# Constants multiplied during TensorE's waits, weight staging moved into the heads' norm, and an output projection in three float32r products

## The chip, the cores and the metric

One core of one Trainium2 chip runs the whole program. The metric is the device time of one execution in microseconds (us). TensorE (PE) multiplies, VectorE (DVE), ScalarE (ACT) and GpSimd (POOL) compute elementwise, SyncE (SP) and also ACT and POOL issue transfers (DMA). TensorE's clock has two levels, 2.4 GHz and 1.2 GHz; the profile's PEclk is the granted share, 1.00 for the first and 0.50 for the second.

## What is computed

Two blocks, one after the other, in float32, on one sequence of 512 tokens of width 1024.

```python
# first block
proj = rmsnorm(x, attn_norm_g) @ w_in
sb_out = stick_breaking_attention(q, k, v)           # 8 heads of 64
d_out = differential_attention(rope(norm(dq)), rope(norm(dk)), dv, lam)   # 4 heads of 2 x 64
d_out = rmsnorm(d_out, diff_subln_g, 1e-5) * 0.8     # norm of each head: lambda_init is 0.2
x = x + concatenate([sb_out, d_out]) @ w_o
h2 = rmsnorm(x, ffn_norm_g)
x = x + (silu(h2 @ w_gate) * (h2 @ w_up)) @ w_down   # hidden width 2816
# second block, on 16 meta tokens and the 512 of x
proj = rms_norm(h) @ w_in_2                          # 72 tiles of 1024 x 128, and dt
branch_conf = silu(layer_norm(conv31(a * sigmoid(g)))) @ w_conf_out
branch_ssm = rms_norm(bidir_ssd(silu(conv7(xbc)), dt) * silu(z)) @ w_ssm_out
h = h + (gate1 * branch_conf + gate2 * branch_ssm) @ w_out
h = h + expert_choice_ffn(rms_norm(h))               # 16 experts, 66 tokens each
out = rms_norm(h[16:])
```

## The kernel before

The order on every engine is written out by hand: a block of Python for each engine issues its instructions one after the other, and semaphores tie them together. An engine works strictly in its written order, so whatever stands behind a waiting instruction waits too.

**A product in float32r.** Most dense products split both operands into a high part (rounded to float32r by an ACT copy) and a low part (raw minus high, by DVE), and TensorE multiplies high by high, high by low and low by high: three passes of one matmul each. `ffn_high` and `ffn_low` do this for the pieces of `w_gate`, `w_up` and `w_down`; `split_piece` (L783, L784, L787) multiplies them. The output projection `wo` (L758) still multiplies plain float32: 8 output tiles m by 8 tiles k, 64 matmuls of 512 columns, from the ring slots 2 and 3 that hold `w_o`, and `MIX`, the heads' outputs.

**Attention.** The stick-breaking heads run as a pipeline over i: scores (L598) of head i, the sums over later keys `("c", i-1)` (L687), the rotation of a rope tile (L699), the output `("o", i-2)` (L714). Between them ACT takes logarithms, DVE subtracts (L1895), POOL masks (L2443) and makes the cosine part (L2456). Then 4 differential heads of 4 query blocks run through scores (L672), softmax on DVE and ACT, transposes (L727) and outputs (L737). Then comes the norm of each head: ACT squares (L1387), PE sums with ones (L748, `subln_sum`), ACT takes the root (L1379, L1381, `subln_root`), DVE scales `MIX` (L1947). In this part PE multiplies the four stick-breaking tiles k = 0 to 3 of output tiles m = 0 to 3 between the sums, and waits for the semaphore `mix_ready` before k = 4 to 7.

**Staging of the second block's weights.** 72 tiles of `w_proj` (512 KB each) are read by POOL's queue (`pre_load`, L2477) into one of 3 buffers, split by ACT (`pre_high`, L1413) and DVE (`pre_low`, L1962), and the low part is written to DRAM by POOL's queue (L2484) for later. This is spread over the first block by tables: `PRE_WO` says how many tiles follow each output tile m of the output projection (6 in all), `PRE_GATE` 2 for each of 22 hidden tiles, `PRE_DOWN` after which pieces of `w_down` (22 of the pieces 3 to 31). POOL issues the first three loads once all heads are normed; afterwards it stores tile q and then loads tile q+2 into the buffer of tile q-1, once that one's store has landed. Before the first FFN weight is split, ACT waits for all tiles of `PRE_WO`, since both use the buffers `WF`. SP's queue loads the big weight blocks (2 MB each) into the ring: the first block of `w_gate`/`w_up` once output tile 3 is done, the second once tile 7 is.

**Second block.** `norm_total("n3")` (L583) sums squares, the dt product follows (L828), then the 72 projection tiles (`split_proj`, L841) among the conformer's taps (DVE L2133, L2082, kept in order with ACT's `conf_gate` L1502, L1506), and for each of 4 groups g the scan over 5 chunks c: `ob` (L978), `of` (L983), `yd` (L988), `sf` (L994), `turn_y` (L925). After the last chunk the dense tail begins: `so` (L1023, L1028), `co`, `out`. The expert part (L1155) ends the program.

```python
            for m in range(DT):
                if m < 4:
                    subln_sum(m)
                wo(m, range(0, 4 if m < 4 else DT))
                if m == 3:
                    pe.wait_ge(S("mix_ready"), DIFF_HEADS)
                    for j in range(4):
                        wo(j, range(4, DT))
```

## Time and profile before

| | |
|---|---|
| median of 3 runs | 2572.95 us (2569.82 to 2579.66) |
| the profiled execution's own time | 2572.31 us |
| its span | 2570.3 us |
| mean granted clock of TensorE | 0.978 |
| busy: PE, DVE, ACT, POOL | 2439.2 us (95%), 1607.2 us (63%), 821.3 us (32%), 406.6 us (16%) |

The span runs from the first to the last instruction of the profiled execution. Times in the rows are microseconds from its start. A float32 matmul shows as two records, a float32r one as one, and matmuls overlap in their records, so the rate of a row of matmuls is read from starts or from the chain of work, not from their mean duration. "Idle before" names what ended the wait of an engine.

### The profile page before, as it was taken

Reading aid. Unit: us, or ns where it says so; the run is one execution under the profiler, and the core shown is the slowest. Engines: PE = TensorE matmul, PEld = TensorE weight load, DVE = VectorE, ACT = ScalarE, POOL = GpSimd, SP = SyncE. Lnnn points to the kernel's source line nnn. Section 1 sums busy time; section 2 is a strip of 40 time slices with the busy share of each in tenths; the row PEclk is TensorE's granted clock in tenths of the full one; section 3 lists DMA queues with packets and bytes.
Section 4 is the critical chain, followed back from the end, with each engine's and each line's share of the span. In section 5 each row is a group of like instructions: output and inputs, shape, how many; then the busy total and the mean of one; then the engine's idle time right before and its main releaser. Section 6 shows DMA issues by size and latency. Waiting matters only on the chain.

```text
span 2570.3 us, 41027 instructions
## 1 busy us (share of the span) xinstructions
PE 2439.2 (95%) x17615; PEld 1541.8 (60%) x17615; DVE 1607.2 (63%) x1749; ACT 821.3 (32%) x1361; POOL 406.6 (16%) x423
## 2 busy tenths in 40 slices
PE   8998899999989999999989989999999999999996
PEld 6764468887879898989879973333322333232322
DVE  4346456664538898988484641766666666666664
ACT  3256544443444646464454421000100000000001
POOL 0033012111202212123330400100000000111110
PEclk9999999999989999999989999999999999999998
DMA  5200168878846454546523468999999999999996
GB/s 201 83 33 1 53 233 296 293 280 283 283 168 201 140 199 148 191 154 210 168 94 116 172 254 308 368 410 414 412 412 412 412 412 415 414 413 411 411 412 233
DMA packets 129717, 676.31 MB, mean 263 GB/s; under 512 B 19300, under 2 KB 52068, under 8 KB 100228
## 3 DMA queue, kind: packets, MB, share of 16 engines
q1 hardware_dynamic: 56624, 554.81, 54.3%
q0 software_dynamic: 25632, 88.49, 10.2%
q10 hardware_dynamic: 47284, 30.42, 4.4%
q8 instruction: 140, 2.29, 0.4%
q14 instruction: 37, 0.30, 0.0%
HBM read 618.55 MB, written 55.12 MB: 262 GB/s over the span
## 4 chain that ended last, share of the span: by engine, by line
PE 66%; DMA 19%; DVE 7%; ACT 4%; issue 2%; POOL 1%; ACTq 0%; SPq 0%; POOLq 0%; DVEq 0%
PE PS L1155 24%; DMA expert_ring_high<-w_experts 12%; PE PS L841 11%; PE PS L1023 5%; DMA arena<-w_proj 3%; PE PS L787 3%; PE PS L783 3%; PE PS L784 3%; PE PS L1028 2%; PE PS L758 2%; DMA ring<-ssd_sums 2%; ACT ring L1562 2%; PE PS L687 1%; PE PS L634 1%; PE PS L635 1%
## 5 line engine op out<-in xcount | busy, mean ns | idle before, releaser
L1155 PE MATMUL PS<-expert_ring_high,U 128*32 128x512 f32 x4240 | 472.2, 596 | 17.5 <-DMA expert_ring_high<-w_experts 16.8
L1155 PE MATMUL PS<-expert_ring_low,U 128*32 128x512 f32 x4016 | 447.1, 593 | 10.7 <-DMA expert_ring_low<-w_experts 8.9
L841 PE MATMUL PS<-XH,RINGF 128*128 128x264 f32 x2304 | 392.4, 289 | 1.2 <-ACT arena L1506 1.2
L1155 PEld LDWEIGHTS PS<-expert_ring_high,U 128*32 128x32 f32 x4240 | 136.2, 110 | 328.4 <-issue 302.6
L841 PEld LDWEIGHTS PS<-XH,RINGF 128*128 128x128 f32 x2304 | 324.3, 189 | 9.2 <-issue 6.8
L1155 PEld LDWEIGHTS PS<-expert_ring_low,U 128*32 128x32 f32 x4016 | 128.7, 110 | 309.4 <-issue 289.7
L2349 DVE SCALAR_TENSOR_TENSOR arena<-expert_ring_low,U,arena 128x2048 f32<-128x2048 f32 x134 | 305.7, 2345 | 0.0
L841 PE MATMUL PS<-UH,RINGF 128*128 128x264 f32 x1152 | 233.7, 285 | 0.0
L2082 DVE SCALAR_TENSOR_TENSOR H<-arena,par,H 128x528 f32<-128x528 f32 x240 | 186.7, 821 | 1.3
L841 PEld LDWEIGHTS PS<-UH,RINGF 128*128 128x128 f32 x1152 | 179.4, 189 | 0.0
L2349 DVE SCALAR_TENSOR_TENSOR arena<-expert_ring_high,U,arena 128x2048 f32<-128x2048 f32 x76 | 174.0, 2347 | 0.5
L2588 POOL DMA_INDIRECT residual_rows<-H,scatter_rows x16 | 29.6, 1851 | 849.2 <-DVE H L2380 849.2
L1772 ACT ACTIVATE H<-PS 128x512 f32<-128x512 f32 x32 | 19.1, 597 | 407.0 <-PE PS L1155 407.0
L1962 DVE TENSOR_TENSOR PREL<-arena,PS 128x1024 fp32r<-128x1024 f32 x66 | 80.4, 1219 | 98.8 <-ACT PS L1413 98.6
L783 PE MATMUL PS<-UX,WF 128*128 128x512 f32 x352 | 138.5, 393 | 0.8 <-DVE UX L1818 0.8
L784 PE MATMUL PS<-UX,WF 128*128 128x512 f32 x352 | 137.1, 389 | 0.0
L2133 DVE SCALAR_TENSOR_TENSOR SQ<-arena,par,SQ 128x528 f32<-128x528 f32 x144 | 109.6, 766 | 6.3 <-ACT SQ L1494 3.7
L2496 POOL TENSOR_TENSOR arena<-arena,ring 128x512 f32<-128x512 f32 (+1 forms) x32 | 60.6, 1898 | 317.5 <-ACT arena L1587 257.7
L1782 ACT ACTIVATE SQ<-PS 2x512 f32<-2x512 f32 x32 | 18.9, 591 | 271.6 <-PE PS L1155 271.2
L1413 ACT ACTIVATE PS<-arena 128x1024 fp32r<-128x1024 f32 x66 | 67.7, 1025 | 116.7 <-DMA arena<-w_proj 114.8
L2358 DVE TENSOR_TENSOR H<-H,PS 128x512 f32<-128x512 f32 x32 | 22.0, 688 | 125.4 <-ACT H L1772 87.2
L1397 ACT ACTIVATE WF<-ring 128x1024 fp32r<-128x1024 f32 (+1 forms) x76 | 71.4, 942 | 80.8 <-PE PS L787 80.1
(358 smaller groups left out, 3898.1 us busy)
## 6 DMA issues: line engine op xcount, KB each, us to landing
expert_ring_low<-w_experts SPq DMA_DIRECT2D x96, 2048.0 KB
expert_ring_high<-w_experts SPq DMA_DIRECT2D x96, 2048.0 KB, 30.0
arena<-w_proj POOLq DMA_DIRECT2D x72, 512.0 KB, 5.6
projection_low_parts<-PREL POOLq DMA_DIRECT2D x72, 512.0 KB, 4.2
ring<-w_proj SPq DMA_DIRECT2D x72, 512.0 KB, 3.7
RINGF<-projection_low_parts SPq DMA_DIRECT2D x72, 512.0 KB, 4.6
ring<-w_gu SPq DMA_DIRECT2D x11, 2048.0 KB, 10.2
ring<-ssd_sums ACTq DMA_DIRECT2D x32, 512.0 KB, 8.5
```

Of the source, the lines that this page charges most:

```text
L783: nc.tensor.matmul(PS[:, bank, :], hi[:, k, :], src[:, 0, k0 + k, :], start=(start and k == 0), stop=False)
L784: nc.tensor.matmul(PS[:, bank, :], hi[:, k, :], src[:, 1, k0 + k, :], start=False, stop=False)
L787: last = nc.tensor.matmul(PS[:, bank, :], lo[:, k, :], src[:, 0, k0 + k, :], start=False, stop=(stop and k == n - 1))
L841: last = nc.tensor.matmul(PS[:, banks[i], 0:HT], w[:, k, :], x[:, k, lo:hi], start=start, stop=stop)
L1023: nc.tensor.matmul(PS[:, banks[i], 0:HT], wh[:, k, :], x(k)[:, lo:hi], start=(first and k == 0 and x is high), stop=False)
L1155: mm = nc.tensor.matmul(PS[QUAD * t:QUAD * t + QUAD, bank, :], stat(t), move(t), start=start, stop=stop)
L1397: A(split_high(p), raw(p), ACT.Copy).then_inc(S("weights_high"), 1)
L1413: A(pre_high_place(q), pre_raw(q), ACT.Copy).then_inc(S("pre_high"), 1)
L1962: V_.tensor_tensor(PREL[:, q % STAGE, :], pre_raw(q), pre_high_place(q).bitcast(F32), SUB).then_inc(S("pre_low"), 1)
L2082: ins = V_.scalar_tensor_tensor(acc, CP[:, u % 3, j:j + T2], par[:, w0 + j:w0 + j + 1], acc, MUL, ADD)
L2133: V_.scalar_tensor_tensor(co, xp[:, k:k + T2], par[:, w0 + k:w0 + k + 1], co, MUL, ADD)\
L2349: ins = V_.scalar_tensor_tensor(LACC[:, a, :], w, XG[:, k, a:a + 1], LACC[:, a, :], MUL, ADD)
```

## The change

1. `fill_wait(bank, n, width)` multiplies `ones` by the constants, n times, in plain float32, into a bank that the next real product overwrites. It stands ahead of a wait at: the sums `("c", 0)` and `("c", 7)` (2 of 512 columns each), `("o", 7)`, the first transposes of the differential heads, every one of their 16 outputs (4, 1, 1, 2 of 128 columns by query block), the first norm of a head, `n3` (5 of 512), dt (2 of 512), `sf` of chunk 0 of groups 1 and 2 (4 and 1 of 256), in group 3 `ob` of chunk 0 (3 of 256) and `yd` (3, 0, 0, 4, 8 of 256 by chunk), ahead of the last `turn_y`, the first `so` (4 of 512) and the first `out`. To allow this `open_` (the wait for the bank) moves ahead of the wait for the operand.
2. The output projection becomes three float32r products. ACT and DVE split the 8 tiles of `w_o` in the stick-breaking loop, one for each head, and `MIX` in 8 tiles: k = 0 to 3 in the last differential head, k = 4 to 7 in the heads' norm. Roots of the heads' norm get other rows, since the split tiles lie where they were.
3. Four staged tiles are split in the heads' norm, and `PRE_WO` keeps 6, so 10 tiles come before the FFN; `PRE_DOWN` has 18 instead of 22, and none after pieces 30 and 31. POOL issues the first three loads after the last stick-breaking scores, and for the first 10 tiles it loads tile q+3 right after the store of tile q, once that store has landed.
4. `conf(1, 0)` (one projection tile) moves from behind the dt sums F, TOT and FR to ahead of them.

```diff
+PRE_HEADS = 4
+PRE_WO = [1, 1, 2, 2, 0, 0, 0, 0]
 PRE_GATE = [2] * FFT
+PRE_DOWN = [n for n in range(3, 31) if n % 3 != 0]
+N_PRE_WO = PRE_HEADS + sum(PRE_WO)
...
+            def fill_wait(bank, n, at=0, width=512):
+                for _ in range(n):
+                    nc.tensor.matmul(PS[:, bank, at:at + width], ones, consts[:, 0:width], start=True, stop=True)
...
                 if 1 <= i <= SB_HEADS:
                     h = i - 1
+                    open_(("c", h), 3, 4, 5)
+                    if h in (0, SB_HEADS - 1):
+                        fill_wait(3, 2)
                     pe.wait_ge(S("sp_masked"), 4 * h + 1)
-                    open_(("c", h), 3, 4, 5)
...
             def wo(m, ks):
+                hi, lo = wo_high(m), wo_low(m)
                 if ks.start == 0:
+                    pe.wait_ge(S("weights_low"), WO_W + m + 1)
                     open_(("wo", m), m % 4)
                 for k in ks:
-                    last = nc.tensor.matmul(PS[:, m % 4, :], w[:, k, (m % 4) * P:(m % 4) * P + P], MIX[:, k, :],
-                                            start=(k == 0), stop=(k == DT - 1))
+                    if m == 0:
+                        pe.wait_ge(S("x_low"), MIX_X + k + 1)
+                    nc.tensor.matmul(PS[:, m % 4, :], hi[:, k, :], mix_high(k), start=(k == 0), stop=False)
+                    nc.tensor.matmul(PS[:, m % 4, :], hi[:, k, :], mix_low(k), start=False, stop=False)
+                    last = nc.tensor.matmul(PS[:, m % 4, :], lo[:, k, :], mix_high(k), start=False, stop=(k == DT - 1))
...
# ACT, stick-breaking loop and heads' norm
+                    act.wait_ge(*in_used[23])
+                    A(wo_high(i), wo_raw(i), ACT.Copy).then_inc(S("weights_high"), 1)
...
                 if h >= 1:
                     subln_root(h - 1)
+                    pre_high(1)
             subln_root(DIFF_HEADS - 1)
+            pre_high(PRE_HEADS - DIFF_HEADS + 1)
...
+            for h in range(DIFF_HEADS):
+                act.wait_ge(S("mix_ready"), h + 1)
+                A(mix_high(4 + h), MIX[:, 4 + h, :], ACT.Copy).then_inc(S("x_high"), 1)
...
# DVE, stick-breaking loop and heads' norm
+                    dve.wait_ge(S("weights_high"), WO_W + i + 1)
+                    if i < SB_HEADS - 1:
+                        dve.wait_ge(S("cos_part"), i + 2)
+                    V_.tensor_tensor(wo_low(i), wo_raw(i), wo_high(i).bitcast(F32), SUB).then_inc(S("weights_low"), 1)
...
             for h in range(DIFF_HEADS):
                 dve.wait_ge(S("head_rooted"), 8 + h + 1)
+                R = HEAD_ROOT[h]
                 V_.scalar_tensor_tensor(MIX[:, 4 + h, :], MIX[:, 4 + h, :], small[:, 5:6], R, MUL, MUL).then_inc(S("mix_ready"), 1)
+                if h >= 1:
+                    mix_rest(4 + h - 1)
+                if h < DIFF_HEADS - 1:
+                    pre_low(1)
+            mix_rest(4 + DIFF_HEADS - 1)
+            pre_low(1)
...
# POOL
-            pool.wait_ge(S("mix_ready"), DIFF_HEADS)
+            got(pool, ("z", SB_HEADS - 1))
...
-                if 1 <= q <= N_PROJ - STAGE:
+                if q < N_PRE_WO:
+                    pre_load(q + STAGE)
+                elif N_PRE_WO < q <= N_PROJ - STAGE:
                     pre_load(q + STAGE - 1)
```

`mix_rest(k)` waits for ACT's high part of tile k and subtracts it from `MIX` on DVE.

**DVE in the heads' norm.** Of the kernel before, from the last differential map on (L1947 scales a head, L1962 makes the low part of a staged tile, L1968 adds an output tile to H):

```order
L1931 SCALAR_TENSOR_TENSOR arena<-arena,small 128x512
L1947 SCALAR_TENSOR_TENSOR arena<-arena,small 128x512 x4
L1968 TENSOR_TENSOR H<-H,PS 128x512 x2
L1818 SCALAR_TENSOR_TENSOR UX<-H,par,UX 128x512
L1962 TENSOR_TENSOR PREL<-arena,WF 128x1024
```

Of the change, the same place (L2033 scales a head, L1985 is `mix_rest`, L2027 the low part of a staged tile, L2051 adds to H):

```order
L2006 SCALAR_TENSOR_TENSOR arena<-arena,small 128x512
L2033 SCALAR_TENSOR_TENSOR arena<-arena,small 128x512
L2027 TENSOR_TENSOR PREL<-arena,WF 128x1024
L2033 SCALAR_TENSOR_TENSOR arena<-arena,small 128x512
L1985 TENSOR_TENSOR GX<-arena,GX 128x512
L2027 TENSOR_TENSOR PREL<-arena,WF 128x1024
L2033 SCALAR_TENSOR_TENSOR arena<-arena,small 128x512
L1985 TENSOR_TENSOR GX<-arena,GX 128x512
L2027 TENSOR_TENSOR PREL<-arena,WF 128x1024
L2033 SCALAR_TENSOR_TENSOR arena<-arena,small 128x512
L1985 TENSOR_TENSOR GX<-arena,GX 128x512 x2
L2027 TENSOR_TENSOR PREL<-arena,WF 128x1024
```

The first `mix_rest` stands ahead of the scaling of heads 2 and 3. Its high part comes from ACT, whose order there is:

```order
L1460 ACTIVATE SQ<-arena 128x512
L1439 ACTIVATE arena<-PS,par 128x512
L1441 ACTIVATE arena<-arena 128x512
L1453 ACTIVATE WF<-arena 128x1024
L1439 ACTIVATE arena<-PS,par 128x512
L1441 ACTIVATE arena<-arena 128x512
L1453 ACTIVATE WF<-arena 128x1024
L1481 ACTIVATE GX<-arena 128x512 x4
```

These are the last square, the root of head 2 (L1439, L1441), a staged tile (L1453), the root of head 3, the fourth staged tile, and then the four high parts of `MIX` (L1481).

**DVE at the end of `w_down`.** Of the kernel before, from piece 28 to the norm n3 (L1950 low part of a piece, L2003 and L2005 an output tile into H, L1826 adds a square):

```order
L1950 TENSOR_TENSOR RINGF<-ring,WF 128x6x128
L1950 TENSOR_TENSOR RINGF<-ring,WF 128x5x128
L1962 TENSOR_TENSOR PREL<-arena,PS 128x1024
L2003 TENSOR_TENSOR U<-PS,RS 128x512
L2005 TENSOR_TENSOR H<-H,U 128x512
L1826 TENSOR_TENSOR U<-U,SQ 128x528
```

Of the change, the same place (L2042 the pieces, L2087 and L2089 into H, L1891 the square):

```order
L2027 TENSOR_TENSOR PREL<-arena,PS 128x1024
L2042 TENSOR_TENSOR RINGF<-ring,WF 128x5x128
L2027 TENSOR_TENSOR PREL<-arena,PS 128x1024
L2042 TENSOR_TENSOR RINGF<-ring,WF 128x6x128
L2042 TENSOR_TENSOR RINGF<-ring,WF 128x5x128
L2087 TENSOR_TENSOR U<-PS,RS 128x512
L2089 TENSOR_TENSOR H<-H,U 128x512
```

No staged tile stands any more between the last two pieces and the last three output tiles.

## Rows read from the trace of the kernel before

**Rows 1.** The chain of waits that ended last, on the page: shares of the span.
```profile
PE 66%; DMA 19%; DVE 7%; ACT 4%; issue 2%; POOL 1%; ACTq 0%; SPq 0%; POOLq 0%; DVEq 0%
```

**Rows 2.** Stretches: length, busy PE, weights, DVE, ACT, POOL, PEclk, DMA share, GB/s.
```profile
156.00:180.00 24.00, 21.72 (x72) 12.71 (x72) 15.13 (x16) 12.30 (x10) 14.85 (x23) 0.86 0.00 0
240.00:286.00 46.00, 33.93 (x170) 22.22 (x171) 30.12 (x72) 31.69 (x93) 0.00 (x0) 0.85 0.00 1
299.00:344.00 45.00, 45.00 (x107) 19.96 (x106) 22.12 (x28) 18.64 (x25) 7.69 (x14) 1.00 0.58 210
380.00:400.00 20.00, 20.00 (x89) 16.48 (x88) 13.11 (x14) 10.32 (x12) 3.92 (x8) 1.00 0.85 299
640.00:660.00 20.00, 17.90 (x71) 14.58 (x72) 10.99 (x12) 8.96 (x11) 4.22 (x8) 0.91 0.82 278
700.00:740.00 40.00, 30.91 (x149) 23.02 (x148) 22.73 (x37) 19.27 (x29) 2.51 (x5) 0.87 0.62 226
980.00:1000.00 20.00, 18.03 (x117) 15.70 (x117) 14.17 (x18) 9.30 (x21) 7.26 (x7) 0.91 0.68 204
1240.00:1260.00 20.00, 17.10 (x99) 14.41 (x98) 10.98 (x13) 6.88 (x11) 5.92 (x5) 0.83 0.67 157
1290.00:1312.00 22.00, 14.12 (x71) 9.85 (x69) 11.61 (x17) 20.85 (x53) 9.09 (x8) 0.75 0.03 13
1312.00:1340.00 28.00, 23.73 (x153) 23.47 (x154) 27.75 (x29) 7.76 (x12) 11.82 (x7) 0.77 0.38 150
```

**Rows 3.** Timeline of PE and POOL, stick-breaking loop: start, duration, what, idle before.
```profile
168.60 5.92 PE L687 MATMUL PS<-arena,consts_sb 128*128 128x512 f32 x14 [2.28 <-POOL arena L2443]
...
226.81 3.09 PE L687 MATMUL PS<-arena,consts_sb 128*128 128x512 f32 x14 [2.33 <-POOL arena L2443]
...
160.12 1.76 POOL L2456 TENSOR_TENSOR U<-arena 128x512 f32<-128x512 f32 x1
...
191.23 1.28 POOL L2456 TENSOR_TENSOR U<-arena 128x512 f32<-128x512 f32 x1
```

**Rows 4.** The chain in order of time, output projection: start, duration, records.
```profile
299.29 44.65 PE PS L758 x104
```

**Rows 5.** Timeline of ACT and DVE in the output projection.
```profile
308.12 1.04 ACT L1413 ACTIVATE WF<-arena 128x1024 fp32r<-128x1024 f32 x1
...
326.97 1.06 ACT L1413 ACTIVATE WF<-arena 128x1024 fp32r<-128x1024 f32 x1 [11.95 <-DMA arena<-w_proj]
...
311.09 1.22 DVE L1962 TENSOR_TENSOR PREL<-arena,WF 128x1024 fp32r<-128x1024 f32 x1
...
343.96 0.69 DVE L1968 TENSOR_TENSOR H<-H,PS 128x512 f32<-128x512 f32 x1 [0.42 <-PE PS L758]
...
347.09 0.74 DVE L1818 SCALAR_TENSOR_TENSOR UX<-H,par,UX 128x512 fp32r<-128x512 f32 x1
```

**Rows 6.** Landing times from 300 to 420 us of L2484 (stores), then L2477 (loads).
```profile
DMA to landing us min/median/max: 2.9/4.9/10.7
...
DMA to landing us min/median/max: 3.7/4.9/11.4
```

**Rows 7.** Timeline of PE and DVE, `w_down` to the dt product.
```profile
642.10 0.67 PE L783 MATMUL PS<-GX,WF 128*128 128x512 f32 x1 [2.42 <-ACT WF L1397]
...
718.70 2.10 PE L583 MATMUL PS<-U,consts_sb 128*128 128x264 f32 x4 [6.14 <-DVE U L1826]
723.17 9.50 PE L828 MATMUL PS<-U,arena 128*64 128x264 f32 x32 [2.36 <-DVE U L2012]
...
710.69 1.22 DVE L1962 TENSOR_TENSOR PREL<-arena,PS 128x1024 fp32r<-128x1024 f32 x1 [3.88 <-ACT PS L1413]
```

**Rows 8.** Timeline of ACT, the second conformer gate.
```profile
776.22 0.61 ACT L1502 ACTIVATE RS<-PS 128x528 f32<-128x528 f32 x1 [3.49 <-PE PS L841]
```

**Rows 9.** Timeline of PE, last chunk of the scan and first dense tile.
```profile
1309.71 1.86 PE L988 MATMUL PS<-arena 16*16 16x64 f32 x16 [3.56 <-DVE arena L2064]
...
1332.90 0.81 PE L1023 MATMUL PS<-XH,WH 128*128 128x264 f32 x2 [3.66 <-DVE YTL L2105]
```

More of the change, by code:

```diff
@@ L99 @@
 PAIRS = 4
-PRE_WO = [1, 2, 1, 2, 0, 0, 0, 0]
+PRE_HEADS = 4
+PRE_WO = [1, 1, 2, 2, 0, 0, 0, 0]
 PRE_GATE = [2] * FFT
-PRE_DOWN = [n for n in range(3, 32) if n % 4 != 2]
-N_PRE_WO = sum(PRE_WO)
+PRE_DOWN = [n for n in range(3, 31) if n % 3 != 0]
+N_PRE_WO = PRE_HEADS + sum(PRE_WO)
 assert N_PRE_WO + sum(PRE_GATE) + len(PRE_DOWN) == N_PROJ
-FFN_W = 24
+WO_W = 24
+FFN_W = WO_W + DT
 PROJ_W = FFN_W + 2 * FFT + 32
@@ L281, in program, with mix_high, mix_low, wo_raw @@
         SUMMED = U[:, 4, 0:3 * P]
+        HEAD_ROOT = [QK[:, row, :] for row in (8, 11, 14, 15)]
+        rows = GX[:, :, :, :].rearrange("p a f n -> p (a f) n")
+        MIX_ROW, V_ROW, QK_ROW = 17, 9, 1
+        assert 2 * DT * SEQ + (FBUF + STAGE) * PIECE - DT * T2 == P + 5 * 1280 + (16 - V_ROW) * SEQ
+        def mix_high(k):
+            return rows[:, (2, 3, 5, 6)[k] if k < 4 else V_ROW + k - 4, :]
+        def mix_low(k):
+            return rows[:, MIX_ROW + k, :]
+        def wo_raw(m):
+            return slot(("wo", m // 4))[:, :, (m % 4) * P:(m % 4) * P + P]
+        def wo_high(m):
+            return WI[:, m // 4, m % 4, :].rearrange("p (k n) -> p k n", k=DT)
+        def wo_low(m):
+            return RINGF[:, slot_of[where["wo", m // 4]] - 2, :].rearrange("p (k n) -> p k n", k=DT)[:, :, (m % 4) * P:(m % 4) * P + P]
         def Z(h):
@@ L887, in _ @@
                 fill(last, ("dtT", part))
+            conf(1, 0)
             pe.wait_ge(*freed(("dtT", 0)))
@@ L905, in _ @@
             fill(last, "FR")
-            conf(1, 0)
             conf(1, 1)
@@ L1333, in _ @@
                     log_terms(i)
+                if i < SB_HEADS:
+                    name = ("wo", i // 4)
+                    act.wait_ge(S(f"ring{slot_of[where[name]]}"), landed[name])
+                    act.wait_ge(*in_used[23])
+                    A(wo_high(i), wo_raw(i), ACT.Copy).then_inc(S("weights_high"), 1)
                 if i >= 1:
@@ L1375, in _ @@
                     diff_out((n - 4) // QB - 1)
+                if 12 <= n < 16:
+                    got(act, ("s", 11))
+                    act.wait_ge(*freed(("o", 2 * (n - 12) + 1)))
+                    A(mix_high(n - 12), MIX[:, n - 12, :], ACT.Copy).then_inc(S("x_high"), 1)
             diff_out(DIFF_HEADS - 1)
@@ L1414, in pre_high, with ffn_high, hidden_high @@
                 pre_turn[0] += n
-            act.wait_ge(S("mix_ready"), DIFF_HEADS)
+            for h in range(DIFF_HEADS):
+                act.wait_ge(*freed(("do", h)))
+                if h >= 2:
+                    got(act, ("sl", h - 2))
+                A(SQ[:, h % 2, 0:SEQ], MIX[:, 4 + h, :], ACT.Square).then_inc(S("subln_sq"), 1)
+                if h >= 1:
+                    subln_root(h - 1)
+                    pre_high(1)
+            subln_root(DIFF_HEADS - 1)
+            pre_high(PRE_HEADS - DIFF_HEADS + 1)
+            def ffn_high(p):
+                name = pieces[p][0]
+                act.wait_ge(S(f"ring{slot_of[where[name]]}"), landed[name])
+                if p >= FBUF:
+                    act.wait_ge(*piece_used[p - FBUF])
+                A(split_high(p), raw(p), ACT.Copy).then_inc(S("weights_high"), 1)
+            def hidden_high(m):
+                act.wait_ge(*freed(("up", m)))
+                A(GX[:, 0, m, :], GXL[:, m, :], ACT.Copy).then_inc(S("x_high"), 1)
+            got(act, ("do", DIFF_HEADS - 1))
+            for h in range(DIFF_HEADS):
+                act.wait_ge(S("mix_ready"), h + 1)
+                A(mix_high(4 + h), MIX[:, 4 + h, :], ACT.Copy).then_inc(S("x_high"), 1)
             for m in range(DT):
```

92 lines of the change are left out of this document (50 added, 42 removed).

## The prediction

> **What bounds the kernel now.** The chain of waits comes first [rows 1]: PE holds 66% of it, then DMA 19% and DVE 7%. So one microsecond taken from PE's own work counts where PE has no wait, and nothing where it waits for another engine. Next come stretches of the span with PE's busy time and granted clock [rows 2]. What a low clock can cost is the length times (1 - PEclk): 24 x 0.14 = 3.4 us in the stick-breaking loop, 46 x 0.15 = 6.9 in the differential heads, 1.8 at 640, 5.2 at 700 to 740, 1.8 at 980, 3.4 at 1240, then 5.5 and 6.4 at the end of the scan. That ceiling is 34 us; it includes time in which PE waits anyhow. The output projection (299 to 344) is the opposite: PE is busy without a gap at full clock [rows 2], and the chain runs through it alone [rows 4]. A wait of 2.28 us at 168.6 left PE slow (14 sums in 5.92 us), a wait of 2.33 at 226.8 did not (3.09 us) [rows 3]. [...]
>
> **Prices.** The chain shows 104 records, 52 float32 matmuls of 512 columns, in 44.65 us [rows 4]: 0.859 us each at full clock, so a fill costs 0.86, 0.43 or 0.215 us for 512, 256 or 128 columns. The first FFN stretch has 89 float32r matmuls in 20.00 us without a gap [rows 2]: 0.2247 each. The sum is made against the profiled execution, 2572.31 us, which is 0.6 below the median.
>
> **1. Stick-breaking loop: +0.2.** Ahead of `("c", 0)` 1.7 us of fill stand where PE had little or no wait, and the loop runs in a circle DVE, POOL's mask, PE, so nothing behind absorbs them: +1.7. The slow sums at 168.6 cost 5.92 - 3.09 = 2.8 us [rows 3]; a fill or a shift ahead of them may save them, I take half, -1.5. The splits of `w_o` are 1.04 us of ACT and 1.22 of DVE for each head [rows 5]; ACT and DVE are busy 12.30 and 15.13 of 24 us [rows 2], so idle time covers them; without that cover each costs its whole length. Bounds: -3 (clock kept, fill hidden) and +5 (fill and half the splits on the circle).
>
> **2. Differential heads: -1.7.** PE is busy 33.93 of 46 us, so the clock cost at most 33.93 x 0.15 = 5.0 [rows 2]; DVE (30.12) and ACT (31.69) also bound the stretch. I take -3.0 for the clock, +0.3 for fills that overrun their wait, +1.0 for the splits of `MIX` tiles 0 to 3 on ACT and DVE. Bounds: -5 and 0.
>
> **3. Output projection: -0.5.** 64 x 0.859 = 55.0 us become 192 x 0.2247 = 43.1, a gain of 11.8. It is mostly given back.
> - Of it, 4 x (3.44 - 2.70) = 2.9 lies in the half products between the heads' sums, where PE waits for the norm in any case.
> - The operands of k = 4 to 7 come late. After ACT's fourth staged tile DVE must do 0.7 + 1.2 + 0.75 + 0.7 + 1.2 + 0.75 + 0.7 + 0.7 = 6.7 us (scalings, low parts, staged tiles; durations of 0.69, 1.22 and 0.74 in [rows 5]), in the order that the change's rows show, with the first low part ahead of the scalings of heads 2 and 3. PE could begin k = 4 at about 300.5 and has 2.7 us of work for the four: output tile 0 is full near 307.4, tile 3 near 315.6, tile 7 near 337.1.
> - The FFN then waits for ten staged tiles. POOL issues store q, waits until it has landed, then issues load q + 3. With the least landing of 2.9 us [rows 6] and two issues I estimate 4.3 us a tile. Store 0 goes out near 298, seven stores (0 to 6) take it to 328, load 9 lands 4.9 us later (median [rows 6]): near 333, split by 334.7. Behind that split DVE has, for the FFN's first operands, some 10.7 us (three rounds of H, operand, square and low part, and the last one). So the last operand is ready at 345.4; before it was 347.09 + 0.74 = 347.8 [rows 5]: -2.4. Before, ACT waited 11.95 us for its last staged tile and still had it by 328, and DVE waited for PE by 0.42 only [rows 5], so there the product was the bound; now the staging is.
> - PE stands idle from 337.1 to 345.4, the longest wait of the program's first part, and starts again at the lower clock: about +1.9.
>
> Bounds: -10.5 (all but the restart's part kept) and +17 (rival B).
>
> **4. `w_down`: -2.5.** Behind a staged tile PE waits 2.42 us at 642.1 and the clock falls [rows 7]; 1.8 us is the loss after it [rows 2]. Staged tiles follow 2 of 3 pieces instead of 3 of 4, so ACT gets 1 us in 12 pieces back. Bounds 0 and -4.7 (stall, clock and a little of each piece).
>
> **5. n3 and dt: -5.0.** DVE's staged tile at 710.69 (1.22 us) is gone from between the last piece and the three adds of H. PE has `w_down` finished at 718.70 - 6.14 = 712.56 and starts n3 at 718.70 [rows 7]. The squares could be added by 715.4, but the five fills take 5 x 0.859 = 4.3 and hold PE to 716.8: -1.9. At full clock n3 itself takes 1.0 less. The dt product takes 9.50 for 16 matmuls [rows 7]; at full clock one of 264 columns takes 0.859 x 264/512 = 0.44, and 16 x 0.44 = 7.0: up to -2.4, of which I take 2.1. Bounds -1.9 and -5.5.
>
> **6. `conf(1, 0)` ahead of F, TOT and FR: +0.7.** One tile is 8 tiles k, three passes and two halves of 264 columns, 48 matmuls, 48 x 0.2247 x 264/512 = 5.5 us, by which the sums of dt and all that follows on DVE come later; ACT's second gate stood idle 3.49 us behind PE [rows 8] and takes part of that. I take +2.0 for DVE and ACT, -1.3 for waits of PE that go. Bounds -1 and +2.
>
> **7. Scan: -6.0.** The low clock at 980 gives -1.4 (ceiling 1.8), at 1240 -2.8 (ceiling 3.4) [rows 2]. At 1290 to 1340 PE is busy 14.12 of 22 us and DVE 27.75 of 28: PE waits 3.56 us for DVE ahead of `yd` and 3.66 ahead of `so` [rows 9], and a fill only replaces idle time. There only the slow matmuls behind 1332.9 gain: -1.8. Bounds of the three: 0 and -8.7. The fills cost nothing, since DVE's work covers them; without that cover they are 0.43 each.
>
> The sum is 0.2 - 1.7 - 0.5 - 2.5 - 5.0 + 0.7 - 6.0 = -14.8: 2572.3 - 14.8 = **2557.5 us**.
>
> **The rivals.**
>
> **A, PE stays the bound of the output projection.** If the staged tiles come at the pace of the stores' median and the block loads don't disturb them, the FFN starts when DVE has followed tile 7: the 11.8 us are kept but for 1.3 of restart and late operands, 10.5 in place of 0.5: 2547.5. For it: no gap in 299 to 344, PEclk 1.00 [rows 2]. Against it: ten tiles instead of six have to pass one queue.
>
> **B, staging takes over: slower.** Tiles 6 to 9 pass while SP's queue brings a block of 2 MB. Landings then reach 10.7 and 11.4 us [rows 6]. If four cycles take 10.7 - 1 instead of 4.3 us, the tenth tile is split at 334.7 + 4 x 4.9 = 354 and the FFN's operands stand at 364.7: 17 us behind before, less the 14.3 of the other terms, 2575. The point from which it decides is a split of the tenth tile behind 349; there the sum is nought. The DMA share of 0.58 in this stretch [rows 2] leaves room, which speaks against it. The Trainium skill (DMA: Bandwidth & Descriptors, Issuing engines are not separate DMA queues) says that transfers issued by different engines interleave on the same 16 DMA engines, which would make POOL's tiles wait behind SP's block; the spread of landings here, 2.9 to 10.7 us, fits it.
>
> **C, the fills don't hold the clock.** They are themselves matmuls that start behind a wait. Then the clock gains go (1.5, 3.0, 1.0, 2.1, 1.4, 2.8, 1.8: 13.6 us) and the five fills ahead of n3 take up to twice 4.3 us and hold it back by some 2: 2572.3 - 14.8 + 13.6 + 2 = 2573. For it: PE was at 0.75 in a stretch where it was busy 64% [rows 2]. Against it: 2.33 us of wait did no harm [rows 3].
>
> **D, the splits of `w_o` collide with POOL in the loop.** POOL's L2456 took 1.76 us once and 1.28 at another time [rows 3]. DVE's new split waits for that instruction, but POOL's masks come next and are on the circle. With 0.5 us in each of 7 rounds: +3.5, 2561. The Trainium skill (SBUF — State Buffer, Who interferes with whom) has it that a DVE instruction with both inputs in SBUF contends with a GpSimd instruction that reads SBUF; by that rule this split is such an instruction, and rows of both lengths agree with it.
>
> **How the numbers follow.** Forecast 0.55, A 0.12, B 0.10, C 0.13, D 0.10. The forecast's own range is 2551 to 2564. The range of 2546 to 2576 takes in A, C and D and about half of B. A measurement of this kernel can tell 0.5%, 12.9 us, from no change: faster means below 2560.1, slower above 2585.8. Below it lie two thirds of the forecast (0.36), all of A (0.12) and a little of D (0.04): 0.52. Above 2585.8 lies only the tail of B and of stalls that I haven't seen, 0.05. The rest, 0.43, is no change that can be told.
>
> **What would show it.** Right: PEclk near 1.00 at 240 to 286, 640, 980 and 1240; PE idle 6 to 10 us ahead of the first gate product, ended by DVE, with ACT waiting for `w_proj` before it; short stalls of PE at k = 4 to 7; the n3 sums starting 2 us closer to the end of `w_down` and dt in about 7 us. Wrong: a first gate product that starts earlier than 340 (A) or later than 355 (B); low clock behind the fills (C); longer masks in the loop (D); or the end of the scan becoming shorter although DVE bounds it there.

## The result and the profile after

The changed kernel takes 2583.77 us (median of 17 runs, 2574.39 to 2587.99), the kernel before 2577.81 us (17 runs beside them). The ratio is 1.0027, 95% interval [1.0018, 1.0036]: 7 us slower, about half of what 0.5% would be, and forecast were 15 us less. The profiled execution of the changed kernel took 2580.63 us (span 2578.6), 8.3 us more than that of before.

Stretches of the changed kernel, beside [rows 2] (length, busy PE, weights, DVE, ACT, POOL, PEclk, DMA share, GB/s):

```profile
156.00:180.00 24.00, 21.82 (x76) 12.46 (x75) 17.00 (x18) 14.59 (x13) 14.01 (x22) 0.93 0.00 0
240.00:286.00 46.00, 40.38 (x253) 28.99 (x252) 33.45 (x77) 35.07 (x100) 0.00 (x0) 1.00 0.00 1
299.00:344.00 45.00, 35.09 (x144) 27.77 (x144) 20.83 (x26) 11.21 (x15) 6.87 (x13) 0.93 0.66 224
344.00:360.00 16.00, 7.17 (x18) 5.15 (x19) 11.69 (x15) 8.76 (x12) 2.11 (x4) 0.61 0.60 189
700.00:740.00 40.00, 39.36 (x184) 29.20 (x183) 22.28 (x37) 17.88 (x26) 1.59 (x3) 1.00 0.54 198
1240.00:1260.00 20.00, 19.69 (x137) 17.24 (x136) 10.89 (x13) 10.41 (x24) 1.63 (x2) 1.00 0.61 179
1290.00:1312.00 22.00, 15.10 (x80) 11.16 (x79) 13.11 (x16) 19.47 (x50) 10.91 (x10) 0.88 0.03 13
```

PEclk is 1.00 in the heads, at n3 and in chunk 0 of group 3, as the fills were meant to have it (x5 below shows which of these is their doing). Yet the kernel is slower, and the stretch of the output projection shows the first cause: PE, busy 45.00 of 45 us before, is now busy 35.09, and 7.17 of the 16 us behind.

Marks of PE in both traces show where the time goes (the last high product of the last `co` closes the run of dense tiles `so` and `co`, which PE works through one after the other); the last column is what the stretch since the mark above it has gained or lost.

| mark | before | after | change |
|---|---|---|---|
| first sum of the heads' norm | 285.32 | 283.55 | -1.8 |
| first low product of the FFN (L787, now L825) | 348.45 | 359.40 | +12.7 |
| end of the last gate/up product | 587.00 | 598.84 | +0.9 |
| end of `w_down` | 712.56 | 719.26 | -5.1 |
| end of the dt product | 732.67 | 734.12 | -5.2 |
| first `ob` of group 0 | 850.87 | 853.43 | +1.1 |
| last `ob` of group 3 | 1292.77 | 1294.72 | -0.6 |
| last high product of the last `co` (with UH) | 1462.67 | 1469.29 | +4.7 |
| end of PE | 2549.86 | 2558.41 | +1.9 |

PE's timeline at the start of the FFN (start, duration, what, idle before). The product ends where it was forecast, at 337.1, and then PE waits 13.52 us:

```profile
336.71 0.39 PE L800 MATMUL PS<-GX,RINGF 128*128 128x512 f32 x1
350.62 0.77 PE L821 MATMUL PS<-UX,WF 128*128 128x512 f32 x1 [13.52 <-issue]
```

ACT and DVE at the tenth staged tile. Its transfer lands at 347.12, DVE comes to the last operand of the FFN at 357.58:

```profile
347.12 1.06 ACT L1453 ACTIVATE WF<-arena 128x1024 fp32r<-128x1024 f32 x1 [8.89 <-DMA arena<-w_proj]
...
357.58 0.75 DVE L1883 SCALAR_TENSOR_TENSOR UX<-H,par,UX 128x512 fp32r<-128x512 f32 x1
```

POOL's queue, beside [rows 6] (L2568 stores, L2561 loads): each load waits for the store just issued, so the stores go one at a time, some 6 us apart, and 10 us while a block of 2 MB moves (SP issues one at 315.16 and one at 337.13):

```profile
300.53 0.54 POOL L2568 DMA_DIRECT2D projection_low_parts<-PREL  x1 [7.24 <-DVE PREL L2027]
303.67 0.53 POOL L2561 DMA_DIRECT2D arena<-w_proj  x1 [2.60 <-DMA projection_low_parts<-PREL]
304.18 0.54 POOL L2568 DMA_DIRECT2D projection_low_parts<-PREL  x1
309.87 0.53 POOL L2561 DMA_DIRECT2D arena<-w_proj  x1 [5.15 <-DMA projection_low_parts<-PREL]
...
326.39 0.53 POOL L2561 DMA_DIRECT2D arena<-w_proj  x1 [8.89 <-DMA projection_low_parts<-PREL]
...
338.68 0.53 POOL L2561 DMA_DIRECT2D arena<-w_proj  x1 [5.18 <-DMA projection_low_parts<-PREL]
```

The chain of work in order of time has these landings one behind the other: store 1, which has no load just ahead of it, takes 2.9 us, store 2, half a microsecond behind a load of the same queue, 5.4, store 4, beside the block, 9.1, and load 9 8.4:

```profile
300.53 2.85 DMA projection_low_parts<-PREL
...
304.18 5.40 DMA projection_low_parts<-PREL
...
316.97 9.14 DMA projection_low_parts<-PREL
...
338.68 8.41 DMA arena<-w_proj
```

The second store also waits for DVE: DVE in the heads' norm stands 7.94 us before the first low part of `MIX`, with the second staged tile behind it:

```profile
298.40 0.69 DVE L1985 TENSOR_TENSOR GX<-arena,GX 128x512 fp32r<-128x512 f32 x1 [7.94 <-ACT GX L1481]
299.01 1.22 DVE L2027 TENSOR_TENSOR PREL<-arena,WF 128x1024 fp32r<-128x1024 f32 x1
```

The second cause is at the end of the scan. PE there, beside [rows 9] (L603 is a fill, L1032 is `yd`, L1069 `so`; a float32 fill is two records):

```profile
1299.94 3.68 PE L603 MATMUL PS<-consts_sb 128*128 128x256 f32 x8 [3.34 <-DVE arena L2148]
1303.43 1.92 PE L1032 MATMUL PS<-arena 128*128 128x64 f32 x16
...
1311.58 6.44 PE L603 MATMUL PS<-consts_sb 128*128 128x256 f32 x16 [1.87 <-DVE arena L2148]
1317.95 1.06 PE L1032 MATMUL PS<-arena 16*16 16x64 f32 x16
...
1320.35 3.70 PE L603 MATMUL PS<-consts_sb 128*128 128x512 f32 x8
1323.49 0.81 PE L1069 MATMUL PS<-UH,WH 128*128 128x264 f32 x2
```

DVE at the first of them:

```profile
1298.07 1.22 DVE L2250 TENSOR_TENSOR arena<-ring,PS 128x1024 f32<-128x1024 f32 x1
1299.21 0.68 DVE L2148 TENSOR_TENSOR arena<-arena,PS 128x512 f32<-128x512 f32 x1
```

L2250 writes the operand of `yd`, and L2148, which stands behind it, reads bank 5 and so releases it. The fills go into bank 5. They start at 1299.94, when all that `yd` needs is there, and `yd` at 1303.43. The wait was for the bank, and nothing written into that bank can fill it.

### The profile page after: what moved, and what is told of

It is laid out like the page before. It is cut to its first block, busy times and chain, and to the rows that moved or that the text cites. A ratio compares the mean times of both kernels' runs of the same rounds, so it can differ in the third digit from the quotient of the medians.

```text
span 2578.6 us, 41525 instructions
## 1 busy us (share of the span) xinstructions
PE 2454.8 (95%) x17841; PEld 1569.0 (61%) x17841; DVE 1627.0 (63%) x1765; ACT 833.8 (32%) x1377; POOL 406.0 (16%) x423
## 4 chain that ended last, share of the span: by engine, by line
PE 71%; DMA 16%; DVE 6%; ACT 3%; issue 2%; POOL 2%; ACTq 0%; POOLq 0%; SPq 0%; DVEq 0%
PE PS L1206 25%; PE PS L881 13%; DMA expert_ring_high<-w_experts 10%; PE PS L825 5%; PE PS L821 5%; PE PS L822 5%; PE PS L1069 4%; DMA expert_ring_low<-w_experts 2%; PE PS L1074 2%; DMA ring<-ssd_sums 1%; DMA projection_low_parts<-PREL 1%; ACT ring L1627 1%; PE PS L667 1%; PE PS L663 1%; PE PS L664 1%
## 5 line engine op out<-in xcount | busy, mean ns | idle before, releaser
L2166 DVE SCALAR_TENSOR_TENSOR H<-arena,par,H 128x528 f32<-128x528 f32 x240 | 188.4, 829 | 1.3
L2042 DVE TENSOR_TENSOR RINGF<-ring,WF 128x1024 fp32r<-128x1024 f32 (+1 forms) x76 | 82.4, 1084 | 62.0 <-ACT WF L1472 61.8
L2027 DVE TENSOR_TENSOR PREL<-arena,PS 128x1024 fp32r<-128x1024 f32 x62 | 75.6, 1219 | 39.9 <-ACT PS L1453 39.2
```

The lines of the kernel that those rows point to most:

```text
L2027: V_.tensor_tensor(PREL[:, q % STAGE, :], pre_raw(q), pre_high_place(q).bitcast(F32), SUB).then_inc(S("pre_low"), 1)
L2042: V_.tensor_tensor(split_low(p), raw(p), split_high(p).bitcast(F32), SUB).then_inc(S("weights_low"), 1)
L2166: ins = V_.scalar_tensor_tensor(acc, CP[:, u % 3, j:j + T2], par[:, w0 + j:w0 + j + 1], acc, MUL, ADD)
```

## The experiments

Each kernel was timed in 5 rounds beside the kernel before. x1 to x5 are edits of the changed kernel, the others build on them. Numbers of PE from the traces: start of the FFN's first low product, length of `w_down`, and "late", from the last `ob` to the last high product of the last `co`. Each trace is one execution, and kernels with the same code in a stretch differ there: in eight of them with the same stick-breaking loop it ends between 232.5 and 235.0, and from the first to the last `ob` the changed kernel, x2, x3 and x4 take 440.7 to 443.6 us.

| kernel | ratio to before [95%] | low product | `w_down` | late |
|---|---|---|---|---|
| before | 1 | 348.45 | 125.56 | 169.90 |
| changed | 1.0027 [1.0018, 1.0036] | 359.40 | 120.42 | 174.57 |
| x1 no late fills | 1.0016 [1.0002, 1.0030] | 359.34 | 120.43 | 169.24 |
| x2 scalings first | 1.0009 [0.9995, 1.0024] | 353.24 | 120.42 | 172.86 |
| x3 six tiles | 0.9982 [0.9968, 0.9996] | 343.38 | 120.42 | 173.51 |
| x4 x2 + two stores | 0.9968 [0.9955, 0.9982] | 342.61 | 120.42 | 173.30 |
| x5 no fills | 1.0019 [1.0006, 1.0032] | 361.61 | 120.42 | 169.90 |
| x7 x4 + x1 | 0.9955 [0.9938, 0.9973] | 343.86 | 120.42 | 168.95 |
| x8 x7, six tiles | 0.9936 [0.9915, 0.9956] | 337.64 | 123.07 | 169.34 |
| x9 x7, float32 product | 0.9940 [0.9921, 0.9959] | 346.33 | 120.43 | 169.81 |
| x10 x8, conf back | 0.9940 [0.9922, 0.9958] | 338.81 | 126.94 | 168.95 |
| x11 x10, other table, no c(0) fill | 0.9958 [0.9941, 0.9974] | 335.29 | 136.17 | 168.92 |
| x12 x8, float32 product | 0.9963 [0.9949, 0.9977] | 346.60 | 127.56 | 169.20 |
| x13 x11, fills in bank 0 | 0.9947 [0.9927, 0.9968] | 336.31 | 128.83 | 167.94 |
| x14 x13, ten tiles | 0.9937 [0.9922, 0.9953] | 340.91 | 120.42 | 168.73 |
| x15 x13, eight tiles | 0.9913 [0.9897, 0.9929] | 337.02 | 120.43 | 169.08 |

**x1, the late fills out.**

```diff
-                        fill_wait(5, (3, 0, 0, 4, 8)[c], width=256)
+                        fill_wait(5, (3, 0, 0, 0, 0)[c], width=256)
...
-                    if m == 0:
-                        fill_wait(0, 4)
```

> The changed kernel without three of its fills at the end of the scan: the 4 and 8 of 256 columns ahead of yd in chunks 3 and 4 of group 3, and the 4 of 512 ahead of the first so. Theory 1 (these fills wait for the bank's release, which is the last thing that PE waits for there, so they start when everything is ready and are paid in full): the first so starts about 8 us earlier against the conv tile before it, PE's wait for YTL is back to about 3.7 us, and the whole is 5 to 6 us shorter than the changed kernel, near 2578. Theory 2 (they fill idle time and keep the clock, as predicted): the whole is 0 to 2 us longer than the changed kernel.

Theory 1 holds in the trace. From the dt product to the first `so` it is 583.6 us in place of 589.4, and over the whole of "late" 169.24 in place of 174.57. In the time it is less clear: by the two ratios the kernel gains 2.8 us, not 5 to 6, and the intervals overlap; the scan ahead of the last `ob` is 2.5 us longer in this trace, in code that x1 doesn't touch. "Late" is 172.9 to 174.6 in the four kernels with these fills and 167.9 to 169.9 in the others. The wait for YTL is 3.30 us.

**x2, DVE's order in the heads' norm.**

```diff
-                if h >= 1:
-                    mix_rest(4 + h - 1)
                 if h < DIFF_HEADS - 1:
                     pre_low(1)
-            mix_rest(4 + DIFF_HEADS - 1)
+            for h in range(DIFF_HEADS):
+                mix_rest(4 + h)
             pre_low(1)
```

> The changed kernel with DVE's order in the heads' norm altered: the four scalings with three staged tiles first, then the four low parts of MIX, then the fourth staged tile. Theory 1 (the first low part holds DVE, so the second staged tile is stored at 300.5 in place of some 292, and the chain of stores starts late): store 1 leaves near 292, PE's stalls at k = 5 to 7 go, the tenth staged tile and the first low product of the FFN come about 8 us earlier, whole 7 to 8 us shorter than the changed kernel. Theory 2 (the chain of stores is set by its cycle beside the 2 MB blocks, whose start moves with PE): a gain of 3 us or less.

The second tile's low part is made at 289.56 (299.01 in the changed kernel), but the tenth comes at 342.50 in place of 348.21, so of 9.4 us 5.7 reach the end: the cycle of the stores takes the rest. The low product is 6.2 us earlier. Between the theories, nearer the first; by the ratios the whole gains 4.6 us where 7 to 8 were expected, and the intervals overlap.

**x3, six tiles ahead of the FFN.**

```diff
-PRE_WO = [1, 1, 2, 2, 0, 0, 0, 0]
+PRE_WO = [1, 1, 0, 0, 0, 0, 0, 0]
-PRE_DOWN = [n for n in range(3, 31) if n % 3 != 0]
+PRE_DOWN = [n for n in range(3, 32) if n % 4 != 2]
```

> The changed kernel with 6 staged tiles ahead of the FFN in place of 10 (4 in the heads' norm, 1 behind each of the first two output tiles) and 22 in w_down as before. Theory 1 (ten tiles through POOL's queue are what the FFN waits for): ACT waits for no staged tile after 317, PE has no wait ahead of the first gate product, the first low product starts near 343 in place of 359.4, and w_down gets some 2.5 us longer: 12 to 15 us shorter than the changed kernel, near 2570. Theory 2 (DVE's own work behind the last output tile is what the FFN waits for, the tiles only coincide with it): 4 us or less shorter.

Theory 1: the low product starts at 343.38, 16 us earlier, with the gate product right behind the output projection, and the whole gains 11.6 us by the ratios (12 to 15 expected). `w_down` did not get longer. The four tiles also take DVE's work for them away, 4 x 1.22 us; x4, which keeps all ten, has its low product as early.

**x4, two stores in flight.** On top of x2:

```diff
-                if q < N_PRE_WO:
-                    pre_load(q + STAGE)
-                elif N_PRE_WO < q <= N_PROJ - STAGE:
+                if 1 <= q <= N_PROJ - STAGE:
                     pre_load(q + STAGE - 1)
```

> As the run with the scalings first, and POOL's queue by the rule of before: store q, then load q + 2 once store q - 1 has landed, so that two stores are in flight. Theory 1 (the cycle of 6.4 us a tile comes from waiting for each store by itself): the cycle falls to 4.5 us or less, the tenth tile is split some 10 us earlier than in the run with the scalings first, and the FFN is bound by PE and DVE, the first low product near 345: 5 to 7 us shorter than that run. Theory 2 (the cycle is the 16 DMA engines' share beside the 2 MB blocks): the cycle stays near 6 us and the time within 2 us of that run.

POOL's queue in x4 (L2567 stores, L2560 loads):

```profile
312.42 0.53 POOL L2567 DMA_DIRECT2D projection_low_parts<-PREL  x1 [2.22 <-DVE PREL L2027]
312.94 0.53 POOL L2560 DMA_DIRECT2D arena<-w_proj  x1
317.12 0.53 POOL L2567 DMA_DIRECT2D projection_low_parts<-PREL  x1 [3.65 <-DVE PREL L2027]
321.62 0.53 POOL L2560 DMA_DIRECT2D arena<-w_proj  x1 [3.96 <-DMA projection_low_parts<-PREL]
325.26 0.53 POOL L2567 DMA_DIRECT2D projection_low_parts<-PREL  x1 [3.11 <-DVE PREL L2027]
325.78 0.53 POOL L2560 DMA_DIRECT2D arena<-w_proj  x1
```

The queue now waits for DVE's splits and only once for a store. From store 1 (292.95) to store 9 (333.17) it is 5.0 us a tile; in x2, which differs by this edit alone, 7.2 (292.01 to 349.54), and in the changed kernel 6.8 (300.53 to 355.19). The tenth tile is split at 331.65, 10.9 us earlier than in x2, as Theory 1 has it, with a cycle half a microsecond over what it said. The DMA engines' share is not what made the cycle long apart from the blocks; beside a block a store still takes 8.2 and 8.9 us. The edit changes two things at once: two stores are in flight, and a store now goes out ahead of its load in place of behind one. Away from the blocks a store lands in 2.9 to 3.8 us in x4 and, from store 1 on, in 5.2 to 5.5 in x2. No run separates the two.

**x5, no fills.** `fill_wait` does nothing.

> The changed kernel with every fill removed, all else as it is. Theory 1 (fills that stand in a real wait keep the clock: heads about 2.5 us, n3 and dt about 3, chunk 0 of group 3 about 2.6; those behind a bank's release or with no wait cost 3 at the end of the scan and 1.7 ahead of the sums of c(0)): without them low clock returns at 240 to 286, at 720 and at 1245, and the whole is 2 to 5 us longer than the changed kernel. Theory 2 (fills as a whole are a loss, the clock doesn't answer to them): 3 to 8 us shorter.

In its trace the clock of 242 to 288 is 0.85 again, but in chunk 0 of group 3 it is 1.00 without a fill:

```profile
242.00:288.00 46.00, 34.77 (x174) 23.30 (x175) 31.07 (x72) 34.00 (x95) 0.00 (x0) 0.85 0.00 1
1240.00:1262.00 22.00, 18.98 (x135) 16.42 (x134) 9.70 (x13) 13.65 (x37) 1.55 (x1) 1.00 0.53 164
```

The loop is 1.1 us shorter (232.48 in place of 233.57), the heads 2.5 longer (52.5 and 50.0), and from the end of `w_down` to the end of dt it takes 16.33 us (14.86 with fills). So the fills lose 1.1 in the loop and gain 2.5 in the heads and 1.5 at n3 and dt. "Late" is 169.90 (174.57): there they lose 4.7. From the first to the last `ob` it is 444.9 (441.3), but 2.6 of these 3.6 us lie in group 0, which has no fill. From the first `ob` of group 1 to the last of group 3 it is 315.4 us without fills, 314.5 with them and 315.0 in the kernel before: they gain nothing there that can be told. The ratio, 1.0019 against 1.0027, leaves open which sign all fills together have.

**x7, x4 and x1 together.**

> The changed kernel with the scalings first, two stores in flight, and without the three late fills: the runs x1 and x4 together. If their effects add: 3 us below x4, about 2563, the first low product of the FFN near 342.6 as there, the first so 5 us earlier than there. If the gain at the FFN is taken back by DVE or the DMA later: no better than x4, 2566.

The result is what adding gives, 0.9955 after 0.9968 (3.3 us) and "late" 168.95 in place of 173.30, though the intervals of the two ratios overlap.

**x8, x7 with the tables of x3.**

> As x7, with six staged tiles ahead of the FFN in place of ten and 22 in w_down. Theory 1 (in x4 the tenth tile, split at 331.65, still holds three rounds of DVE's work back): ACT waits for no staged tile after 317, PE's last output tile at 333.5 is the bound, and the first low product comes near 339 in place of 342.6; against it w_down ends with staged tiles behind its last pieces and dt starts 1.9 us later: 1 to 2 us below x7. Theory 2 (DVE's order behind the last output tile bounds both): within 1 us of x7 at the first low product, and 2 us longer as a whole.

The low product is at 337.64, theory 1, with PE's last output product ending at 334.2 and no wait. `w_down` gets 2.7 us longer. The ratio of 0.9936 can't be told from x7's 0.9955.

**x9, the product in float32 again.** In x7, `wo` with the lines of before, the copies and subtractions for `w_o` and `MIX` out.

> As x7, with the output projection in plain float32 again, and without the splits of w_o and of MIX on ACT and DVE. Theory 1 (PE's 11.8 us of saved product are mostly covered by what the FFN waits for: DVE's rounds and the tenth tile): 52 float32 matmuls from about 299 to 344, the first low product of the FFN near 348.5 in place of 342.6, so 5 to 6 us longer than x7. Theory 2 (with the queue mended PE is the bound and the product is worth what it saves on PE behind 299): 8.9 us or more longer than x7. Theory 3 (the splits on ACT and DVE cost the loop and the heads as much as the product gives): within 2 us of x7.

Theory 3 in the time (2561.3 us and 2564.1, intervals overlap), and in the trace a low product only 2.5 us later (346.33). With ten tiles the three passes are worth nothing that can be measured in the time.

**x12, the same with six tiles.** x8 with the float32 product.

> As x8, with the output projection in plain float32 and without its splits, as x9 is to x7. Theory (in x9 the three passes gained only 2.5 us at the first low product since the tenth tile held x7; with six tiles nothing holds it): the first low product at 346 in place of 337.6, 8 to 9 us later than in x8, and the whole 6 to 9 us longer, as far as the FFN's own loads don't take it back. Rival (the splits on ACT and DVE or the FFN's weight loads eat the rest): within 3 us of x8 as a whole.

Here the low product comes at 346.60 in place of 337.64: 9.0 us, as expected, and the time is 2566.47 against 2557.86 us (6.9 us by the ratios, whose intervals overlap). Of that difference `w_down` holds 4.5 us (127.56 against 123.07), and the stretch to dt gives 2.3 back (14.8 against 17.1); the product made neither. At the start of the FFN the product's gain exists once nothing else is late.

**x10 and x11, conf back, then two small edits.**

```diff
# x10, on x8
-            conf(1, 0)
             pe.wait_ge(*freed(("dtT", 0)))
...
             fill(last, "FR")
+            conf(1, 0)
             conf(1, 1)
# x11, on x10
-                    if h in (0, SB_HEADS - 1):
+                    if h == SB_HEADS - 1:
                         fill_wait(3, 2)
-PRE_DOWN = [n for n in range(3, 32) if n % 4 != 2]
+PRE_DOWN = [n for n in range(3, 30) if n % 5 != 2]
```

> As x8, with conf(1, 0) behind F, TOT and FR again. Theory (by the traces, the earlier tile makes PE wait 4.4 us for ACT's gate at one place in place of 1.25 us there and 1.7 in two others, and the clock falls after it): the wait of 4.4 us and the low clock behind it go, the first back state (L978) comes about 1 us earlier measured from the dt product, whole 1 us shorter than x8. Rival (the move pays for itself): 0 to 2 us longer than x8, waits of PE for DVE and POOL return.

> As x10, also without the two fills ahead of the sums of c(0), and with the 22 staged tiles of w_down behind pieces 3 to 29 only. Theory (both are small and add): the loop 1.7 us shorter, n3's sums 1.9 us closer to the end of w_down, whole 3 to 4 us below x10, near 2553. Rival for the fill (it keeps the clock behind 170): low clock after the wait at 170 and no gain in the loop. Rival for the tiles (w_down gets slower by what n3 gains): w_down 1 to 2 us longer.

The waits answer as the theory says: in x8 PE waits 4.40 us for ACT's gate at 762.14, in x10 1.25 us. But from dt to the first `ob` it is 118.2 us in before, x11 and x13, 119.8 in x10, 119.7 and 119.6 in x14 and x15 and 119.1 to 120.2 in the ten others with the early tile: a microsecond at most, and not settled. As a whole x10 (0.9940) can't be told from x8 (0.9936). In x11 the sums of c(1) start at 169.29, 1.5 us earlier than in x10, with low clock behind them still. The new table misses: `w_down` takes 136.17 us, and the whole is 2566.00 us where 2553 were expected. The staged tiles land late there, ACT waits for them (1.03 us is the copy) and PE for ACT:

```profile
667.62 1.03 ACT L1451 ACTIVATE PS<-arena 128x1024 fp32r<-128x1024 f32 x1 [6.77 <-DMA arena<-w_proj]
...
669.47 0.79 PE L821 MATMUL PS<-GX,WF 128*128 128x512 f32 x1 [4.86 <-ACT WF L1470]
```

**x13, fills where they can run.** On x11:

```diff
+                    if g == GROUPS - 1 and c >= 3:
+                        pe.wait_ge(*freed(last_tag[0]))
+                        fill_wait(0, 4)
                     open_(("yd", g, c), 5)
```

> As x11, with 4 fills of 512 columns each ahead of yd in chunks 3 and 4 of group 3, in bank 0, whose last reader is long done, and ahead of the wait for yd's own bank. Theory (the fills of the changed kernel cost time only because their bank came free last): the fills run inside the waits of 3.6 and 4.3 us, yd starts within 0.3 us of its time in x11, the low clock behind 1296 goes, and the whole is 1 to 3 us shorter. Rival (a fill there delays yd whatever the bank, or the stretch is DVE's and the clock is worth nothing): 0 to 3 us longer.

PE in x13 (L603 the fills, L1035 `yd`):

```profile
1278.22 1.02 PE L1025 MATMUL PS<-arena 128*128 128x512 f32 x2
1279.08 3.59 PE L603 MATMUL PS<-consts_sb 128*128 128x512 f32 x8
1282.51 1.89 PE L1035 MATMUL PS<-arena 128*128 128x64 f32 x16
```

The stretch around it, of x11 and then of x13:

```profile
1284.00:1319.00 35.00, 28.46 (x159) 22.43 (x158) 25.59 (x31) 26.27 (x58) 15.73 (x12) 0.76 0.25 97
```

```profile
1277.00:1312.00 35.00, 31.19 (x185) 22.45 (x184) 27.58 (x32) 25.30 (x52) 16.36 (x12) 1.00 0.31 121
```

The fill starts right behind `of` and `yd` follows 4.29 us after that matmul's start, in x11 4.48 (1286.42 to 1290.90) without a fill: it costs nothing there, and the clock is 1.00 in place of 0.76. The second group of fills (1288.09) is over before the bank of `yd` comes free: PE waits another 1.72 us for DVE. In the changed kernel half as many columns, in bank 5, held `yd` back by 3.5 us (1299.94 to 1303.43). What the clock gives back is little, since the wait for YTL behind stays at 3.68 us: "late" is 167.94 to 169.08 in x13 to x15 against 168.92 in x11. Most of x13's lead over x11 as a whole is `w_down` (128.83 against 136.17). The ratios of the two, 0.9947 and 0.9958, can't be told apart.

**x14 and x15, how many tiles where.** x13 with the tables of the changed kernel, and with eight tiles:

```diff
+PRE_WO = [1, 1, 1, 1, 0, 0, 0, 0]
+PRE_DOWN = [n for n in range(3, 31) if n % 7 not in (2, 5)]
```

> As x13, with ten staged tiles ahead of the FFN and 18 in w_down, as in the changed kernel. It asks what the smaller number in w_down is worth. Theory (staged tiles that land late stop w_down; so far 117.9 us in each trace with 18 of them, and 117.9, 119.6, 122.6, 123.0, 124.4, 125.0 and 130.0 with 22): w_down takes 117.9 us again with no wait of PE over 1 us, 4 to 5 us less than in x13, and the first low product of the FFN comes 7 us later than in x13: the whole 2 to 3 us longer than x13. Rival (the waits in w_down are chance, not number): w_down within 1 us of x13 or with waits as there.

> As x13, with eight staged tiles ahead of the FFN (4 in the heads' norm, 1 behind each of the first four output tiles) and 20 in w_down. Theory (with two stores in flight eight tiles pass before PE has finished the output projection, near 324): the first low product of the FFN within 1 us of x13, w_down 118 to 121 us, the whole 2 to 4 us below x13 and the fastest of all, 2557 to 2560. Rival (the eighth tile holds DVE as the tenth did): the first low product 3 us later or more than in x13.

The lengths of 117.9 and so on in the first expectation count from the first low product of `w_down`; the table above counts from the end of the last gate product. With 18 staged tiles `w_down` takes 120.42 or 120.43 us in all eight traces that have 18, with 20 in x15 too, and with 22 it is 120.42 once and 123 to 136 six times, the kernel before among them. So with 18 or 20 tiles no trace has a stall, with 22 six of seven have one, and its length changes from trace to trace. Which pieces the tiles follow differs too (x11 and x13 have 22 behind 27 pieces), and no run tells number from place. x14 has its first low product 4.6 us later than x13 and a `w_down` 8.4 us shorter, and as a whole the two can't be told apart (0.9937 and 0.9947). x15 has both: no wait in `w_down` and the first low product at 337.02. At 0.9913 [0.9897, 0.9929] and 2554.69 us against 2576.21 it has the lowest ratio, 22 us below before, and by the two ratios some 29 below the changed kernel; its interval still touches those of x8, x13 and x14.

## Why the prediction was wrong

**Step 3, the output projection, failed by size, and most of the miss is there.** Forecast -0.5, measured +12.7: 13 of the 23 us between -14.8 and +8.3. PE's part was right (end forecast 337.1, measured 337.10), and what stands behind the split of the tenth tile to 2 us (10.7 forecast, 8.9 measured). What was mis-sized is the cycle of POOL's queue: "I estimate 4.3 us a tile", from the least landing in [rows 6]. Between stores 1 and 7 it was 6.4 (300.53 to 339.20). The tenth load was issued at 338.68, not 328, and took 8.4 us to land, not 4.9: the tile was split at 349, not 334.7. The 2.9 us came true for store 1, which has no load just ahead of it (its cycle is 3.65 us); behind a load of the same queue a store took 5.3 to 5.8, and beside the block 9.1. The median of the same rows, 4.9 us, with two issues of 0.53 would have given 6.0. That is rival B at its deciding point, 349, held to be 1 in 10 though its rows were there. (B's sum has a slip of its own: 9.7 in place of 4.3 is 5.4 us a cycle, not 4.9, which gives a split at 356 and 2577 us.)

**Step 7, the end of the scan, failed in its mechanism.** "A fill only replaces idle time" was said with [rows 9] in hand, and these rows name L2064 as what ended the wait: the instruction that reads bank 5, not L2166, which writes the operand. The fills wait for the same bank. That "DVE's work covers them" was misread as well: DVE's 27.75 of 28 us belong to 1312 to 1340, while at 1290 to 1312, where `yd` waits, DVE is busy 11.61 of 22. Forecast -1.8 for this end, measured +4.7, of which x1 takes 5.3 away. The fill ahead of the first `so` stood at 1313, where PE had no wait at all; the 3.66 us wait of [rows 9] is for YTL, 20 us later.

**The other parts of step 7** were forecast -4.2; from the first to the last `ob` it is -0.6. The clock is 1.00 at 980 and 1240, as forecast, but x5 has 1.00 at both places too, without a fill. At the second it had waits of 1.60 and 1.42 us just before; in the kernel before, the clock fell behind 1.50 and 1.39. Chunk 0 of group 3 takes 17.6 us in place of 20.8, and it takes 17.6 in x5 as well. The fills ahead of `sf` are paid in full: chunk 0 of group 1 takes 11.75 us with them and 10.02 without, and chunks 0 and 1 together 22.8 against 22.1 in x5. So the size forecast for these fills isn't borne out, and what makes the low clock come or stay away in the scan is open.

**Step 5 was right**: -5.0 forecast, -5.2 measured, the fills hold PE to 723.39 and dt takes 7.3 us (7.0 forecast). x5 splits it: 3.8 us stay without fills.

**Step 4 was right in sign**, -2.5 against -5.1, just outside its bound of -4.7: the lower rate of staged tiles doesn't save ACT a microsecond here and there, it removes every stall. The nine traces with 18 or 20 tiles show it; one with 22, x3, has none either.

**Steps 1, 2 and 6**: -1.5 forecast for loop and heads together, -1.8 measured: +0.8 in the loop (+0.2 forecast) and -2.6 in the heads (-1.7), with PEclk 1.00 from 240 to 286 as forecast. The sums behind 170 ran partly slow (4.44 us, between the 5.92 and 3.09 of [rows 3]). conf: +0.7 forecast, +1.1 measured. The last 1.9 us, behind the dense tiles `so` and `co`, are in code that the change hardly touches; that length is 1086.4 to 1090.6 in all these traces.

**Rivals.** C was wrong in the heads and at n3, where the clock is low in the kernel before and in x5 (0.85 in the heads) and 0.96 to 1.00 in the kernels with the fills; in the scan x5 leaves it open, and at the end x13 against x11 speaks for the fills, with one trace each. D came true once and cost nothing that shows: in the last round of the loop, beside DVE's split at 227.41, a POOL addition takes 1.33 us in place of 0.45, and 0.45 again in x9 and x12, which have no split. A did not come true in the changed kernel, since its condition failed; x8 against x12 shows that its price was about right: once the tiles are out of the way, the product is worth 9.0 us at the FFN's start.
